# Two mixer layers and a hybrid block on one core: token projections 512 columns wide over chunk pairs, attention steps from small to large, tiles at multiples of 2048 bytes

## The reference, cut to what matters

```python
h = rms_norm(x, norm_g[l]) * (1.0 + scale) + shift
proj = h @ w_in[l]                       # gq gk gv | glr | gz | dq dk dv dz
gqkv = silu(causal_depthwise_conv([gq, gk, gv], conv_w[l]))
o_gla = gla_branch(...)                  # chunks of 64, state per head, then rms_norm * silu(gz)
# diff_branch, for each block of 128 queries and each of 4 heads:
s = einsum('bqhmd,bkhmd->bhmqk', q, k)   # two maps m, keys up to the query's chunk of 64
p = softmax(where(mask, s, -inf))
attn = p[:, :, 0] - lam * p[:, :, 1]
o_diff = rms_norm(attn @ v, g_out) * (1 - lam_init) * silu(dz)
x = x + gate * ([o_gla, o_diff] @ w_out[l])
```

## Time and profile before

| | us |
|---|---|
| median of 3 runs | 1782.62 (1779.47 to 1783.09) |
| the profiled execution | 1783.18 |
| its span, first to last instruction | 1781.4 |
| mean granted TensorE clock, share of 2.4 GHz | 0.992 |
| PE busy | 1737.3 |
| DVE, ACT, POOL busy | 760.9, 650.9, 736.9 |

### The profile page before, as it was taken

How to read it: one execution, slowest core, us unless ns; L and a number is a source line. 1 busy time by engine, 2 the same in 40 slices (tenths; PEclk the granted TensorE clock), 3 DMA queues, 4 the chain that set the end, 5 groups by cost and what they waited for, 6 DMA issues and landing times.

```text
span 1781.4 us, 23044 instructions
## 1 busy us (share of the span) xinstructions
PE 1737.3 (98%) x9041; PEld 1440.5 (81%) x9041; DVE 760.9 (43%) x896; ACT 650.9 (37%) x812; POOL 736.9 (41%) x315
## 2 busy tenths in 40 slices
PE   4999999899999999999999999999999999999997
PEld 2687898688898888888889988888888888888885
DVE  3656656765656533332332524651113533333122
ACT  4333564344555433333333422232222433333221
POOL 2233233334323544444444444444444454444442
PEclk8999999999999999999999999999999999999998
DMA  8542114221111222222223322222222222222221
GB/s 343 204 165 98 55 54 183 69 73 72 62 58 72 95 94 94 94 96 87 98 96 102 113 97 100 89 92 95 94 94 95 95 95 97 102 104 75 95 94 70
DMA packets 30749, 180.80 MB, mean 101 GB/s; under 512 B 4406, under 2 KB 4540, under 8 KB 14172
## 3 DMA queue, kind: packets, MB, share of 16 engines
q1 hardware_dynamic: 24480, 161.50, 25.6%
q10 hardware_dynamic: 6204, 18.39, 2.9%
HBM read 177.78 MB, written 2.10 MB: 101 GB/s over the span
## 4 chain that ended last, share of the span: by engine, by line
PE 92%; DVE 3%; ACT 2%; DMA 2%; issue 1%; SPq 0%; DVEq 0%; ACTq 0%
PE ps L940 25%; PE ps L942 24%; PE ps L941 24%; PE ps L976 4%; PE ps L978 3%; PE ps L977 3%; DMA ada_w<-w_ada 2%; PE ps L1176 1%; PE ps L1198 1%; PE ps L1057 1%; PE ps L1209 0%; PE ps L1185 0%; PE ps L1019 0%; PE ps L1022 0%; PE ps L1021 0%
## 5 line engine op out<-in xcount | busy, mean ns | idle before, releaser
L523 POOL TENSOR_TENSOR wl<-raw,wh 128x1024 fp32r<-128x1024 f32 (+1 forms) x304 | 735.0, 2439 | 1019.2 <-ACT wh L568 1019.2
L940 PE MATMUL ps<-xh,wh 128*128 128x512 f32 x1280 | 505.0, 395 | 8.3 <-DVE xl L1489 4.3
L941 PE MATMUL ps<-xl,wh 128*128 128x512 f32 x1280 | 500.2, 391 | 0.0
L942 PE MATMUL ps<-xh,wl 128*128 128x512 f32 x1280 | 499.8, 390 | 0.0
L568 ACT ACTIVATE wh<-raw 128x2048 fp32r<-128x2048 f32 x152 | 291.3, 1916 | 550.2 <-PE ps L942 513.3
L940 PEld LDWEIGHTS ps<-xh,wh 128*128 128x128 f32 x1280 | 241.4, 189 | 68.0 <-issue 16.3
L942 PEld LDWEIGHTS ps<-xh,wl 128*128 128x128 f32 x1280 | 241.4, 189 | 50.7
L941 PEld LDWEIGHTS ps<-xl,wh 128*128 128x128 f32 x1280 | 241.5, 189 | 49.7 <-issue 0.5
L976 PE MATMUL ps<-wh,xh 128*128 128x256 f32 x576 | 168.5, 293 | 0.0
L978 PE MATMUL ps<-wl,xh 128*128 128x256 f32 x576 | 162.9, 283 | 0.0
L977 PE MATMUL ps<-wh,xl 128*128 128x256 f32 x576 | 162.8, 283 | 0.0
(11 more groups left out here) (256 smaller groups left out, 2039.3 us busy)
## 6 DMA issues: line engine op xcount, KB each, us to landing
raw<-ffn_in_stream SPq DMA_DIRECT2D x44, 1024.0 KB, 4.8
raw<-mixer_stream SPq DMA_DIRECT2D x40, 1024.0 KB, 4.8
raw<-layer_stream SPq DMA_DIRECT2D x36, 1024.0 KB, 4.8
raw<-ffn_out_stream SPq DMA_DIRECT2D x32, 704.0 KB, 4.1
ada_late<-w_ada ACTq DMA_DIRECT2D x24, 512.0 KB, 4.6
ada_w<-w_ada SPq DMA_DIRECT2D x8, 1024.0 KB, 18.8
gate_w<-w_ada ACTq DMA_DIRECT2D x4, 1024.0 KB, 9.9
x<-x_t SPq DMA_DIRECT2D x1, 2048.0 KB, 7.7
```

Of the source, the lines that this page charges most:

```text
L523: last = nc.gpsimd.tensor_tensor(wl[u][:, cols], raw[u][:, cols], wh[u][:, cols].bitcast(F32), ALU.subtract)
L940: nc.tensor.matmul(bank_ap, w0, x0, start=first, stop=False)
L941: nc.tensor.matmul(bank_ap, w0, x1, start=False, stop=False)
L942: return nc.tensor.matmul(bank_ap, w1, x0, start=False, stop=last)
```

## The change

Three things.

**Pairs.** In k, v and z two chunks are used at once: raw, wh and wl of both buffers become one tile each with a middle dimension of 2 (the halves 8192 bytes apart), and a matmul moves 2 x 256 columns, one strip of each chunk, into a whole bank. A unit is now two token blocks (u = 0: blocks 0 and 1, u = 1: blocks 2 and 3) over both chunks, one block in bank 0 and one in bank 1; a part is 2 of the 8 k-tiles for both blocks, 2 x 2 x 3 = 12 matmuls. Both banks are complete only with part 3. PE waits for the unit before's banks at part 0 only.

**Quarters.** Both chunks are needed from the first to the last unit of a pair, so wh and wl of the next pair are written behind PE: when an odd unit has done part f < 3, ACT copies quarter f of both chunks (`next_quarter`, 1024 elements), POOL subtracts it; quarter 3 follows behind the two emptyings at part 3. Ahead of k and v, whose predecessors conv and q use one chunk at a time, ACT copies halves of single chunks (`half_high`). q and the first two output units get their weights by this way too, as pairs. POOL frees both raw tiles at once, with the last quarter.

**Attention upwards.** The query block rises from 0 to 3, so that steps of 128 keys come first and those of 512 last (n = 47 to 50); the first steps need only the first token blocks of v.

**Places.** Small tiles come first, then x to wl, then the arena, all at multiples of 2048; u_in goes to the end of the layer's tiles, and states, mix_h[0] and mix_l[0] with it. In the mixer v2_sq and tpad share other tiles' room.

```diff
-ALIGN = 128
+ALIGN = 2048
...
-            put(36 + s, "diff_ss", 3 - (s - 6) // 4)
+            put(36 + s, "diff_ss", (s - 6) // 4)
...
+PAIR0, PAIRS, TURNED_PAIRS = L_CONV, 6, (0, 2)
+QW = CW // 4
...
-    qb, h = TB - 1 - s // HEADS, s % HEADS
+    qb, h = s // HEADS, s % HEADS
...
+        raw_both = sb("raw_both", [P, 2, CW])
+        wh_both = sb("wh_both", [P, 2, CW], F32R)
+        wl_both = sb("wl_both", [P, 2, CW], F32R)
+        raw, wh, wl = ([both[:, u] for u in range(2)] for both in (raw_both, wh_both, wl_both))
...
-        mix_h = [at(f"mix_h{g}", [P, HEADS, S], F32R, (arena, at_conv + KT * S * 4)[g]) for g in range(2)]
+        mix_h = [at(f"mix_h{g}", [P, HEADS, S], F32R, (at_u, at_conv + KT * S * 4)[g]) for g in range(2)]
...
+            def split_pair(n, separate):
+
+                for f in range(4):
+                    cols = slice(f * QW, f * QW + QW)
+                    pool.wait_ge(quarter_high[0], 4 * n + f + 1)
+                    if separate:
+                        pool.wait_ge(quarter_high[1], 4 * (n // PAIRS * len(TURNED_PAIRS)
+                                                           + TURNED_PAIRS.index(n % PAIRS)) + f + 1)
+                    last = nc.gpsimd.tensor_tensor(wl_both[:, :, cols], raw_both[:, :, cols],
+                                                   wh_both[:, :, cols].bitcast(F32), ALU.subtract)
+                    if f % 2 == 0:
+                        last.then_inc(quarter_low, 1)
+                    else:
+                        last.then_inc(half_split if f == 1 else w_ready, 2)
...
                     last = (stage, j) == ("z", L_Z - 1)
-                    if t and not last:
+                    if t and stage == "conv" and j < 2:
                         take_high(unit + 2)
...
+                        tb, c0 = 2 * (j % 2) + t, j // 2 * WIDTH
+                        dst = {"k": k_tok, "v": v, "z": zg}[stage][:, tb, c0:c0 + WIDTH]
+                    if t == 0 and stage in ("conv", "q") and unit >= unit0 + 2:
+                        half_high(unit + 2, t)
                     nc.scalar.activation(dst, bank, func).then_inc(banks_free[u], 1)
-                    if t and last:
-                        take_high(unit + 2)
+                    if t == 1 and stage in ("conv", "q") and unit >= unit0 + 2:
+                        half_high(unit + 2, t)
+
+                def half_high(chunk, half):
+
+                    u = chunk % 2
+                    cols = slice(2 * half * QW, 2 * half * QW + 2 * QW)
+                    act.wait_ge(raw_landed[u], 16 * (chunk // 2) + 16)
+                    nc.scalar.activation(wh[u][:, cols], raw[u][:, cols], ACT.Copy).then_inc(quarter_high[u], 2)
+
+                def next_quarter(unit, f):
+
+                    if f < 3:
+                        used = (unit - unit0 - PAIR0) // 2
+                        act.wait_ge(quarter_used, 3 * (4 * l + (0, None, 1, 2, 3)[used]) + f + 1)
+                    cols = slice(f * QW, f * QW + QW)
+                    for u in range(2):
+                        act.wait_ge(raw_landed[u], 16 * ((unit + 1) // 2) + 16)
+                    nc.scalar.activation(wh_both[:, :, cols], raw_both[:, :, cols], ACT.Copy
+                                         ).then_inc(quarter_high[0], 1)
...
+                        kind, j, p = at_
+                        if kind in ("conv", "q"):
+                            if p % 2:
+                                empty(kind, j, p // 2)
+                            continue
+                        if p == 3:
+                            empty(kind, j, 0)
+                            empty(kind, j, 1)
+                        if j % 2:
+                            next_quarter(unit0 + PART0[kind] + j, p)
...
+                    if u == 0:
+                        pair_ready(unit, p)
+                    for b in range(2):
+                        if p == 0:
+                            pe.wait_ge(banks_free[(unit - 1) % 2], emptied(unit - 1, b))
+                        last = token_steps(2 * u + b, b, (2 * p, 2 * p + 1))
+                        if p == 3:
+                            last.then_inc(tile_done, 1)
+                    if u and p < 3:
+                        last.then_inc(quarter_used, 1)
...
+                def pair_ready(chunk, f):
+
+                    n = l * PAIRS + (chunk - unit0 - PAIR0) // 2
+                    if f % 2 == 0:
+                        pe.wait_ge(quarter_low, 2 * n + f // 2 + 1)
                     else:
-                        if p == 0:
-                            chunk_ready(0, unit, 0)
-                        last = token_block(u, p, 0)
-                    if half:
-                        last.then_inc(tile_done, 1)
+                        pe.wait_ge(half_split if f == 1 else w_ready, chunk + 2)
+
+                def token_steps(tb, bank, ks):
+
+                    cols = slice(tb * P, tb * P + P)
+                    dst = ps[:, bank].rearrange("p (a c) -> p a c", a=2)
+                    for k in ks:
+                        w = slice(k * 256, k * 256 + 256)
+                        nc.tensor.matmul(dst, xh[:, k, cols], wh_both[:, :, w], start=(k == 0), stop=False)
+                        nc.tensor.matmul(dst, xl[:, k, cols], wh_both[:, :, w], start=False, stop=False)
+                        last = nc.tensor.matmul(dst, xh[:, k, cols], wl_both[:, :, w], start=False, stop=(k == KT - 1))
+                    return last
```

More of the change, by code:

```diff
@@ L276, in build @@
         o_diff = place("o_diff", [P, TB, WIDTH])
+        at_u = cursor[0]
+        u_in = place("u_in", [P, KT, S + CONV_K - 1])
         ss_k = place("ss_k", [P, TB, 8])
@@ L338, in build @@
         half_used = sem("half_used")
+        quarter_high = [sem(f"quarter_high{u}") for u in range(2)]
+        quarter_low = sem("quarter_low")
+        quarter_used = sem("quarter_used")
         tile_done = sem("tile_done")
@@ L478, in _ @@
                     u = k // 5
-                    sp.dma_start(raw[u][:], ins["layer0_stream"][u]).then_inc(raw_landed[u], 16)
+                    sp.dma_start(raw[u], ins["layer0_stream"][u]).then_inc(raw_landed[u], 16)
             def load_pair(dram, size, i, chunk):
@@ L516, in _, with split @@
                                     pattern=[[-1, P]], channel_multiplier=1).then_inc(pool_step, 1)
-            def split(size, i, chunk, u):
-                pool.wait_ge(w_high, i * 2 + (chunk + u + 1))
+            def split(size, i, chunk, plain, u):
+                pool.wait_ge(w_high, i * 2 + (plain + u + 1))
                 for half in range(2):
@@ L525, in split @@
                     last.then_inc(half_split if half == 0 else w_ready, 1)
[L527 to L530, removed]
-                        split(size, i, chunk, u)
-                chunk += count
+            def split_pair(n, separate):
[11 more added lines that the diff above has]
+                        last.then_inc(half_split if f == 1 else w_ready, 2)
+            chunk = plain = 0
+            for n, (_, count, size) in enumerate(segments):
+                runs = ((0, PAIR0), (PAIR0 + 2 * PAIRS, L_UNITS)) if n < LAYERS else ((0, count),)
+                for c0, c1 in runs:
+                    if n < LAYERS and c0:
+                        for pair in range(PAIRS):
+                            split_pair(n * PAIRS + pair, pair in TURNED_PAIRS)
+                    with pool.Fori(0, (c1 - c0) // 2) as i:
+                        for u in range(2):
+                            split(size, i, chunk, plain, u)
+                    plain += c1 - c0
         N_CONST = 10
@@ L1127, in part @@
                         return
-                    if half == 0:
-                        pe.wait_ge(banks_free[(unit - 1) % 2], emptied(unit - 1, t))
                     if stage in ("conv", "q"):
+                        if half == 0:
+                            pe.wait_ge(banks_free[(unit - 1) % 2], emptied(unit - 1, t))
                         if half == 0:
@@ L1701, in gated_z @@
                     dve.wait_ge(z_act, 2 * l + g + 1)
-                    if g:
-                        copied("z", L_Z - 1, tb // 2)
+                    if g and tb >= 2:
+                        copied("z", L_Z - 1, tb % 2)
                     nc.vector.tensor_tensor(o[g][:, tb], zg[:, tb, g * WIDTH:(g + 1) * WIDTH], o[g][:, tb], ALU.mult
```

52 lines of the change are left out of this document (24 added, 28 removed).

## The result

The changed kernel takes **1786.56 us** (median of 12 runs, 1783.16 to 1787.37), the one before 1781.47 in as many runs beside it (1779.09 to 1783.58): **ratio 1.0023, 95% interval 1.0015 to 1.0030**: 4.1 us slower by the ratio, 5.1 by the medians. The profiled execution has a span of 1784.5 us at a mean granted clock of 0.991.

The account below looks back on a forecast made before the run. The prediction took the issue rate of PE's matmuls as the bound. 1783.2 - 7.7 - 1.4 + 2.8 = 1776.9, less 0.56 for the median, gave about 1776.5 us, range 1769 to 1788.

Parts of the forecast that it names:

- The wide matmuls: Token parts of k, v, z: 12 matmuls of 512 columns instead of 24 of 256, 7.7 us saved.
- rival D: A moving operand in two strips costs as two matmuls, so the 7.7 us is gone: 1784.2 us; chance 0.12.
- The places: Matmuls on mix_h[1] and mix_l[1] and the low-rank ones get faster through alignment: 1.4 us saved.
- Rival B: Absolute alignment speeds every matmul, another 6.5 ns on at least 4896 of 512 columns: 32 us, 1745 us; chance 0.12.
- Quarters ... Covered: Behind token units, each quarter is copied and subtracted before PE wants it: 4 us against 11.4 or more.
- No backlog should form ... No stall: In attention, ScalarE frees bank 0 at 4.7 us, before PE comes for it at 4.8: no stop.
- The end of the layer: Output units wait 0.7 us on mix_l, 1.1 on the last quarter; 1.4 lost a layer, 2.8 in all.
- Rival C: ScalarE keeps a 6.1 us lag at four attention boundaries, freeing banks late: 8.0 us a layer, 1792 us; chance 0.10.

Follow-up runs that it names:

- e9: Changed kernel with both stops removed (nbias, gated_r and layer-end order edited), its 512-column token matmuls cut into two of 256: 1777.55 us, ratio 0.9975 to the kernel before.
- e6: Kernel before with only the new places of its tiles: 1779.46 us against 1781.57, ratio 0.9991.
- e8: Changed kernel with large tiles from a multiple of 128 bytes instead of 2048: 1787.07 us, ratio 1.0031 to the kernel before.
- e3: Changed kernel with nbias from two one-tensor operations and first-half gated_r moved to attention steps 5 to 8: 1777.30 us, ratio 0.9973 to the kernel before.
- e1: Changed kernel with nbias made by two operations reading one SBUF tensor and a scalar each: 1777.29 us against 1782.48 for the kernel before, ratio 0.9970.
- e10: Changed kernel with smax of the 128 to 384 key steps written to PSUM, nbias still one operation: 1775.74 us, ratio 0.9969 to the kernel before.
- e11: Kernel before with attention upwards, and second-half gated_r and gated_z alternating by token block: 1779.64 us against 1782.33, ratio 0.9985.

## Why the prediction was wrong

The time lies inside the stated range, but on the wrong side: 6 us less was forecast, and 4 to 5 us more came out; more than 3.6 us slower had a chance of 0.12.

- **The wide matmuls, -7.7 us: right.** Parts of 2.86 us; e9 gives 7.5. Two strips cost nothing; rival D falls. 7.5 us over 64 x 12 = 768 matmuls is 9.8 ns for each one saved. The 2.5 ns over the columns that the Trainium skill gives ("TensorE: Matmul & The Clock Gate", Back-to-back issue gap; there for a matmul isolated from others) would have given 1.9 us, an estimate from that page.
- **The places, -1.4 us: right by the pitch.** 0.233 to 0.227; 1.1 us in e6's layers. Rival B falls, by the FFNs' unchanged pitch (0.227 before and after) and by e8.
- **"Quarters ... Covered": the step that failed.** I asked whether each quarter is ready in time, and in the changed kernel it was. I did not ask what POOL's 2.4 us do to DVE, nor see that steps 1 to 3 would each have a quarter beside their nbias. The first stop, 2.5 us a layer and 1.7 behind it, comes from that. The kernel before showed it: there too nbias took 1.72 us at 187.44 with a subtraction from 186.75 to 189.14, and gated_z of the second half 6.90 us against 2.50 unhindered in e3. I read the DVE rows of a step for their usual lengths and not for their longest. Timelines of DVE and POOL in the kernel before:

```profile
187.44 1.72 DVE L1714 TENSOR_TENSOR nbias<-smax,nrq 128x2 f32<-128x2 f32 x1
...
275.75 6.90 DVE L1704 TENSOR_TENSOR o_diff<-zg,o_diff 128x512 f32<-128x512 f32 x4
```

```profile
186.75 4.73 POOL L523 TENSOR_TENSOR wl<-raw,wh 128x1024 fp32r<-128x1024 f32 x2 [12.37 <-ACT wh L568]
```

- **"No backlog should form ... No stall" (bank hand-over): wrong by that.** 2.5 us after the score, I said; 6.3 were measured in step 3. My 2.5 was read from the step's first score and my 6.1 for 512 keys from its last; from the first, step 3 took 6.5. The room was real: with nbias unhindered (e1, e10) PE doesn't stop there. One boundary of the four stopped, the one behind the steps of 128 keys; the last had 0.3 us.
- **The end of the layer, 2.8 us lost: place and order right, size wrong.** I had mix_l 0.7 us late and the last quarter 1.1. mix_l was 2.4 us late. I followed ACT's row of work and did not price DVE's gated_z (6.90 us, not 3.01), which sits ahead of the head sums and by the trace makes 1.5 of the 2.4. The last quarter was no stop of its own in the changed kernel, where the half clock covers it; in e3 and e10 it is one of 1.0 us, as predicted.
- **The clock: not in the sum.** Four stretches of 3.4 us at half clock cost 4 x 1.7 = 6.8 us together, behind stops of 9.7.
- **The sum again**, for the layers: parts -7.0, places -1.1, stops +9.7, clock +6.8, together +8.4; measured 513.1 - 506.9 = +6.2. The 2.2 between are near the 2.6 by which e11 is shorter than the kernel before; that they are the same is not shown. Rival C had the slower side and one of its places, but for another reason: it is not ScalarE's own backlog.

## What to carry to other kernels

Before work on GpSimd that reads SBUF is cut finer or tied to another engine's step, list the VectorE instructions with two SBUF inputs that can stand beside it: any of them, a product of two columns too, can cost the whole of the GpSimd instruction. Look at the longest of a line, not at its mean, and see whether its end coincides with one of GpSimd's. Where one sits on the path, give it an input in PSUM or a scalar pointer, or run it ahead of what sets GpSimd off; in an order written by hand 0.1 us decides whether it is caught.

## What the runs showed that I had not expected

In the layers of all twelve traces PE stopped 18 times for 2.4 to 2.9 us from one matmul's start to the next (idle for 2.1 to 2.5). In 12 of the 18 a stretch of 3.4 us at half clock went with it: in all four of the changed kernel, in none of e3's and e10's two each at the first output tile, though these were 2.75 us long. By the first stop, such a stop costs 2.5 us or 4.2; what decides it, these runs don't tell.

A tiny instruction pays the whole lock: 128 x 2 elements took 2.37 us. And it works both ways: in the changed kernel the quarter that began at 199.86, beside a gated_r begun at 199.78, took 2.83 us on POOL instead of 2.37.
